# Decoder trunk step on one core: x turned on TensorE before its norm is known, the first head's work first, u and v rows by turns

## The reference

```python
xn = rms_norm(x, g_mix)
z = xn @ w_in                                  # q_a k_a v_a q_b k_b v_b g_a g_b
oa, ob, state = mix_fn(...)                    # dilated and sliding-window attention, with rotary
merged = sigmoid(ga) * (oa @ w_a) + sigmoid(gb) * (ob @ w_b)
h = x + merged @ w_o
hn = rms_norm(h, g_ffn)
# PEER, for each position and each of 8 heads:
q = (hn @ w_q)                                 # two halves of 128
s = q . sub_keys                               # 2 x 128 scores
# top 16 of each half, top 16 of their sums -> 16 experts e, gates = softmax
act = gelu(hn . u_tab[e])                      # 128 rows of 1024 per position
out = sum_e (gates * act)[e] * v_tab[e]
y = rms_norm(h + out, norm_final)
```

## Time and profile before

| | |
|---|---|
| runs, median | 2101.64 us |
| profiled execution, its own time | 2102.63 us |
| its span | 2100.8 us |
| busy: PE / DVE / GpSimd (POOL) / ACT | 1467.6 / 1215.2 / 1151.1 / 359.8 us |
| moved by DMA | 713.80 MB, mean 340 GB/s |
| share of DMA engine time: GpSimd's queue / SP's queue | 78.2% / 13.7% |
| the chain that ended last: PE / issue / DMA / POOL / DVE | 27% / 24% / 15% / 14% / 13% |

### The profile page before, as it was taken

How to read it: one execution, slowest core, us unless ns; L and a number is a source line. 1 busy time by engine, 2 the same in 40 slices (tenths; PEclk the granted TensorE clock), 3 DMA queues, 4 the chain that set the end, 5 groups by cost and what they waited for, 6 DMA issues and landing times.

```text
span 2100.8 us, 18792 instructions
## 1 busy us (share of the span) xinstructions
PE 1467.6 (70%) x5438; PEld 665.6 (32%) x5438; DVE 1215.2 (58%) x3337; ACT 359.8 (17%) x901; POOL 1151.1 (55%) x1082
## 2 busy tenths in 40 slices
PE   5999898954976687668985666664566576645457
PEld 4444344443432244333332222222222233211111
DVE  2015342287767467667644767767666767876440
ACT  2112342222221122211100111211112111100000
POOL 3020000045656657666666767677777677767664
PEclk9999999965997888778898778787877778867869
DMA  9979976578999989998999999989999999999997
GB/s 319 379 276 366 360 275 217 166 253 297 361 399 345 366 274 388 346 381 315 400 395 407 354 343 361 338 336 361 357 354 354 348 354 336 358 391 367 380 342 274
DMA packets 230423, 713.80 MB, mean 340 GB/s; under 512 B 21336, under 2 KB 49912, under 8 KB 230296
## 3 DMA queue, kind: packets, MB, share of 16 engines
q0 software_dynamic: 166912, 612.40, 78.2%
q1 hardware_dynamic: 63408, 100.19, 13.7%
HBM read 707.99 MB, written 72.65 MB: 372 GB/s over the span
## 4 chain that ended last, share of the span: by engine, by line
PE 27%; issue 24%; DMA 15%; POOL 14%; DVE 13%; another core or an unknown queue 3%; ACT 2%; POOLq 1%; SPq 0%; DVEq 0%; ACTq 0%
POOL WR L606 7%; PE bank L975 6%; DMA XS<-in_peer_u_dram,e_all 5%; DMA arena<-in_peer_u_dram,e_all 5%; POOL XS L606 5%; PE bank L866 4%; DVE XS L1363 4%; PE bank L992 4%; PE bank L1070 3%; DMA WR<-in_peer_v_dram,arena 3%; POOL arena L606 2%; PE bank L1111 2%; PE bank L1091 1%; DMA WR<-out_dram 1%
## 5 line engine op out<-in xcount | busy, mean ns | idle before, releaser
L975 PE MATMUL bank<-WR,arena 128*64 128x512 f32 x2048 | 654.4, 746 | 332.7 <-DMA WR<-in_peer_v_dram,arena 252.0
L606 POOL DMA_INDIRECT WR<-in_peer_v_dram,arena x512 | 564.0, 1101 | 277.5 <-issue 169.3
L1363 DVE SCALAR_TENSOR_TENSOR XS<-XS,GT 128x1024 f32<-128x1024 f32 x384 | 465.4, 1225 | 334.2 <-DMA XS<-in_peer_u_dram,e_all 292.1
L606 POOL DMA_INDIRECT XS<-in_peer_u_dram,e_all x384 | 419.1, 1091 | 317.5 <-issue 119.4
L975 PEld LDWEIGHTS bank<-WR,arena 128*64 128x64 f32 x2048 | 181.7, 166 | 742.2 <-issue 703.5
L1363 DVE SCALAR_TENSOR_TENSOR arena<-arena,GT 128x1024 f32<-128x1024 f32 x128 | 157.0, 1226 | 24.9 <-DMA arena<-in_peer_u_dram,e_all 18.6
L606 POOL DMA_INDIRECT arena<-in_peer_u_dram,e_all x128 | 121.8, 951 | 42.7 <-issue 37.5
L992 PE MATMUL bank<-WR,XS 128*128 128x512 f32 x256 | 117.3, 612 | 12.2 <-ACT GT L732 11.8
L866 PE MATMUL bank<-WR,XS 128*128 128x512 f32 x256 | 112.0, 595 | 0.0
L679 ACT ACTIVATE XS<-bank 128x256 f32<-128x256 f32 (+1 forms) x90 | 36.0, 404 | 425.5 <-remote 215.9
L1111 PE MATMUL bank<-XS,GT 128*128 128x128 f32 x608 | 86.7, 306 | 24.8 <-DVEq L1278 10.3
(11 more groups left out here) (208 smaller groups left out, 1679.4 us busy)
## 6 DMA issues: line engine op xcount, KB each, us to landing
out_dram<-in_cache_a_k_dram POOLq DMA_DIRECT2D x8, 4064.0 KB, 52.1
out_dram<-in_cache_a_v_dram POOLq DMA_DIRECT2D x8, 4064.0 KB, 51.9
GT<-in_w_peer_q_dram SPq DMA_DIRECT2D x17, 1024.0 KB, 8.3
WR<-in_w_in_dram SPq DMA_DIRECT2D x8, 2048.0 KB, 24.4
WR<-in_w_out_dram SPq DMA_DIRECT2D x6, 2048.0 KB
WR<-in_peer_v_dram,arena POOLq DMA_INDIRECT x512
WR<-in_w_branch_a_dram SPq DMA_DIRECT2D x6, 1024.0 KB
WR<-in_w_branch_b_dram SPq DMA_DIRECT2D x6, 1024.0 KB
```

Source lines behind the costliest of these rows:

```text
L606: nc.gpsimd.indirect_dma_start(dst, None, table, bass.IndirectOffsetOnAxis(ap=idx, axis=0))\
L975: last = nc.tensor.matmul(b[c][R * j:R * j + R, :], diag[v % 4][:, s % 4, :], V[V_AT[s]][:, c * CHUNK:(c + 1) * CHUNK], start=False, stop= ...
L1363: V_.scalar_tensor_tensor(u, u, 1.0, hidden[q // TILE_Q], ALU.mult, ALU.mult, accum_out=dots[:, s // TOPK % 4, s % TOPK:s % TOPK + 1]).the ...
```

## The change

Three things are changed.

1. ACT squares each tile of x when it lands, and PE transposes the unscaled x, all five tiles before the first projection. `rstd` is applied as the scale of ACT's evacuations instead of by DVE on x. The identity, tile 0 and `gmix` are loaded first. `sel` is copied later.
2. In steps 21 to 28 the pieces of the first choice (`CHAIN`) come first in each step. The attention of tile 1 moves to steps 25 to 28 (its `turned` stays on step 21, its `first` goes to 24), the decode rows' values are spread anew (20, 20, 25, 26, 27, 27, 28, 29), `sample_back` and `sample_own` go two steps later, and `lists`, `sums`, `pick`, `spread`, `weigh` and `index` of the very first head one step earlier. SP's loads of values and query weights are reordered to match.
3. GpSimd asks for u and v rows by turns.

```diff
@@ -71,7 +71,8 @@
     for i in range(TILES * NH):
-        x = i if i < NH else SLOT0 - NH // 2 + i - NH
+
+        x = i if i < NH else (25, 26, 26, 27, 27, 28, 28, 28)[i - NH] if i < NH + 8 else SLOT0 - 8 + i - NH
         t, hd = divmod(i, NH)
...
@@ -82,9 +83,9 @@
         elif hd == 0:
-            put(x, "turned", t)
+            put(x if t > 1 else 21, "turned", t)
             put(x if t > 1 else NH, "post", t - 1)
-            put(x, "first", t)
+            put(x if t > 1 else 24, "first", t)
         if hd == HA + 1:
...
@@ -96,12 +97,12 @@
         put(2 * b, "sample_qk", b)
-        put(20 + b, "sample_pv", b)
+        put((20, 20, 25, 26, 27, 27, 28, 29)[b], "sample_pv", b)
     put(15, "sample_soft")
     put(16, "sample_norm")
     put(17, "sample_turn")
-    put(28, "sample_back")
-    put(29, "sample_own")
+    put(30, "sample_back")
+    put(31, "sample_own")
     put(SLOT0 + 41, "post", TILES - 1)
...
@@ -120,7 +121,7 @@
                     continue
-                put(x + lag, stage, t, h)
+                put(x + lag - ((t, h) == (0, 0) and lag >= 2), stage, t, h)
     put(head_at(SAMPLE, PH - 1) + 8, "sample_turn_lists")
...
@@ -152,6 +153,8 @@
             rest.append(p)
+    if beside == "chain":
+        return sorted(pieces, key=lambda p: 0 if p[0] in CHAIN else 1)
     if beside:
...
@@ -162,15 +165,21 @@
 
+CHAIN = ("square", "norm", "hidden", "query", "query_out", "score", "score_out", "lists", "sums", "pick")
+
 
 def beside(x, pieces):
 
     names = [p[0] for p in pieces]
+    if SLOT0 - 8 <= x < SLOT0:
+        return "chain"
     return x >= SLOT0 - NH // 2 and names.count("att") <= 1 and "first" not in names and "end" not in names
 
 
 def other_order(pieces, beside):
 
+    if beside == "chain":
+        return sorted(pieces, key=lambda p: 0 if p[0] in CHAIN else 1)
     return sorted(pieces, key=lambda p: 3 if beside and p[0] in ATT else FIRST.get(p[0], 2))
...
@@ -387,12 +397,13 @@
         def _(sp):
-            for t in range(TILES):
-                sp.dma_start(GT[:, t, 0:D], x_p[t * P:(t + 1) * P, :]).then_inc(S["x_in"], 16)
+            sp.dma_start(ident[:, :], ident_d).then_inc(S["id_in"], 16)
+            sp.dma_start(GT[:, 0, 0:D], x_p[0:P, :]).then_inc(x_in[0], 16)
+            sp.dma_start(gmix[:, :], g_mix.rearrange("(k p) -> p k", p=P), allow_slow_non_contiguous=True).then_inc(S["id_in"], 16)
+            for t in range(1, TILES):
+                sp.dma_start(GT[:, t, 0:D], x_p[t * P:(t + 1) * P, :]).then_inc(x_in[t], 16)
             sp.wait_ge(S["x_zero"], 1)
-            sp.dma_start(GT[0:DEC, SAMPLE, 0:D], x_s).then_inc(S["x_in"], 16)
-            sp.dma_start(ident[:, :], ident_d).then_inc(S["id_in"], 16)
-            sp.dma_start(gmix[:, :], g_mix.rearrange("(k p) -> p k", p=P), allow_slow_non_contiguous=True).then_inc(S["id_in"], 16)
+            sp.dma_start(GT[0:DEC, SAMPLE, 0:D], x_s).then_inc(x_in[SAMPLE], 16)
             sp.dma_start(w_ring[1][:, :, 0:2 * WK], w_in_v[:, :, KB:KB + 2 * WK]).then_inc(S["w_in1"], 16)
...
@@ -518,11 +529,14 @@
             branch_weights(1, 1)
-            for b in range(3, 7):
-                values(b)
+            values(3)
+            values(4)
             query_weights(1)
+            values(5)
+            values(6)
+            query_weights(2)
             values(7)
-            for n in range(2, 6):
+            for n in range(3, 6):
                 query_weights(n)
...
@@ -643,26 +657,27 @@
                         q = piece[1]
-                        if q < UQ:
-                            for j in range(QUAD):
+                        for j in range(QUAD):
+                            if q < UQ:
                                 fetch_u(q * QUAD + j)
-                        if LAG <= q < UQ + LAG:
-                            for j in range(QUAD):
+                            if LAG <= q < UQ + LAG:
                                 fetch_v((q - LAG) * QUAD + j)
 
         @block.scalar
         def _(act):
-            act.wait_ge(S["x_in"], XLOADS)
             act.wait_ge(S["eps"], 1)
             for t in range(ALL):
+                act.wait_ge(x_in[t], 16)
                 nc.scalar.activation(GT[:, t, D:2 * D], GT[:, t, 0:D], ACT.Square, accum_out=ss[:, t:t + 1])\
                     .then_inc(S["stat"], 1)
             act.wait_ge(S["stat"], ALL)
             nc.scalar.activation(std, ss, ACT.Sqrt, bias=epsc, scale=1.0 / D).then_inc(S["std"], 1)
 
+            act.wait_ge(S["rstd"], 1)
             for m in range(ALL):
                 act.wait_ge(full[2 + m], 1)
-                nc.scalar.activation(Z[:, m, KB:KB + 2 * WK], bank[2 + m][:, 0:2 * WK], ACT.Copy).then_inc(free[2 + m], 1)
+                nc.scalar.activation(Z[:, m, KB:KB + 2 * WK], bank[2 + m][:, 0:2 * WK], ACT.Copy, scale=rstd[:, m:m + 1])\
+                    .then_inc(free[2 + m], 1)
 
...
@@ -671,8 +686,8 @@
                     act.wait_ge(full[2 + m], 2 + c if m < TILES else 3 + 2 * c)
-                    nc.scalar.activation(Z[0:n, m, CHUNK_AT[c]:CHUNK_AT[c] + CHUNK], bank[2 + m][0:n, :], ACT.Copy)\
-                        .then_inc(free[2 + m], 1)
+                    nc.scalar.activation(Z[0:n, m, CHUNK_AT[c]:CHUNK_AT[c] + CHUNK], bank[2 + m][0:n, :], ACT.Copy,
+                                         scale=rstd[0:n, m:m + 1]).then_inc(free[2 + m], 1)
 
...
@@ -827,12 +844,12 @@
             def transpose_x(m):
-                pe.wait_ge(S["xs"], m + 1)
+                pe.wait_ge(x_in[m], 16)
                 for half in range(2):
                     if m:
                         pe.wait_ge(free[half], m)
                     for k in range(4):
-                        col = D + (4 * half + k) * P
+                        col = (4 * half + k) * P
                         last = nc.tensor.transpose(bank[half][:, k * P:(k + 1) * P], GT[:, m, col:col + P], ident[:, :])
...
@@ -844,11 +861,9 @@
 
-            pe.wait_ge(S["sel"], 4)
-            transpose_x(0)
             for m in range(ALL):
-                if m + 1 < ALL:
-                    transpose_x(m + 1)
+                transpose_x(m)
+            for m in range(ALL):
                 pe.wait_ge(free[0], m + 1)
...
@@ -867,6 +882,8 @@
                     if m == 0:
+                        if c == 0:
+                            pe.wait_ge(S["sel"], 4)
                         pe.wait_ge(free[2 + SAMPLE], 2 + 2 * c)
...
@@ -1136,14 +1153,7 @@
 
-            dve.wait_ge(S["std"], 1)
-            V_.reciprocal(rstd, std).then_inc(S["rstd"], 1)
-            dve.wait_ge(S["rstd"], 1)
-            for t in range(ALL):
-                V_.tensor_scalar(GT[:, t, D:2 * D], GT[:, t, 0:D], rstd[:, t:t + 1], None, ALU.mult).then_inc(S["xs"], 1)
             dve.wait_ge(S["id_in"], 32)
-            for j in range(4):
-                V_.tensor_copy(sel[32 * j:32 * j + 32, :], ident[32 * j:32 * j + 32, 32 * j:32 * j + DEC]).then_inc(S["sel"], 1)
             for m in range(ALL):
...
@@ -1151,6 +1161,10 @@
                         .then_inc(free[half], 1)
+            dve.wait_ge(S["std"], 1)
+            V_.reciprocal(rstd, std).then_inc(S["rstd"], 1)
+            for j in range(4):
+                V_.tensor_copy(sel[32 * j:32 * j + 32, :], ident[32 * j:32 * j + 32, 32 * j:32 * j + DEC]).then_inc(S["sel"], 1)
             for e in range(G):
```

More of the change, by code:

```diff
@@ L337, in hybrid_step_kernel @@
         free = [sem(f"free{i}") for i in range(8)]
-        for n in ("x_in", "const_in", "w_in0", "w_in1", "ab_in0", "ab_in1", "out_in0", "out_in1", "wq0_in", "gffn_in", "gfin_in",
-                  "x_zero", "copies", "stat", "std", "rstd", "xs", "rot", "rot_s", "probs", "pv", "onorm", "merged",
+        for n in ("const_in", "w_in0", "w_in1", "ab_in0", "ab_in1", "out_in0", "out_in1", "wq0_in", "gffn_in", "gfin_in",
+                  "x_zero", "copies", "stat", "std", "rstd", "rot", "rot_s", "probs", "pv", "onorm", "merged",
                   "dve", "kvzero", "q_out", "kv_in0", "kv_in1", "q_in0", "q_in1", "v_in0", "v_in1", "v_in2",
@@ L346, in hybrid_step_kernel @@
         stored = [sem(f"stored{t}") for t in range(TILES)]
+        x_in = [sem(f"x_in{t}") for t in range(ALL)]
         u_landed = [sem(f"u_landed{j}") for j in range(UR)]
@@ L361, in hybrid_step_kernel @@
         CHUNK_AT = [QA, KA, VA, QB] + [ZW + c * CHUNK for c in range(4)]
-        XLOADS, CONSTS = 16 * ALL, 16 * 14
+        CONSTS = 16 * 14
         Z_ORDER = (SAMPLE, 0, 1, 2, 3)
@@ L731, in _ @@
                         b = filled(act, "gate", at[0], 0)
-                        nc.scalar.activation(GT[:, m, c * CHUNK:(c + 1) * CHUNK], b[:, :], ACT.Sigmoid if m < TILES else ACT.Copy)\
+                        nc.scalar.activation(GT[:, m, c * CHUNK:(c + 1) * CHUNK], b[:, :], ACT.Sigmoid if m < TILES else ACT.Copy,
+                                             scale=rstd[:, m:m + 1] if m < TILES else 1.0)\
                             .then_inc(free[misc_bank("gate", at[0], 0)], 1)
@@ L736, in _ @@
```

(3 more changed lines are left out.)

## The result

The kernel after takes 2212.73 us (median of 4 runs, 2201.27 to 2217.31) where the kernel before, on the same chip, takes 2104.48 (4 runs, 2100.76 to 2109.02). The ratio is 1.0505, 95% interval 1.0454 to 1.0556: 108 us slower, where 2083 was forecast. The profiled execution took 2208.53 us, with a span of 2206.7.

The account below looks back on a forecast made before the run. Expert row fetching near the DMA limit was taken to bound three quarters of the span, PE's way to the first choice the start. 2100.8 - 12 - 12 + 5 = 2081.8, plus 1.8 outside, less 1.0 for the median: 2083; range 2048 to 2113.

Parts of the forecast that it names:

- Part 1: Start of the kernel, x turned as it lands: PE reaches the 512-column matmuls 12 us earlier, bounds 8 and 15.
- give-back of 0 to 4: Weight loads beside the cache copies may use up spare time: -4 to 0 us of the early start, kept for the range.
- Part 2: First choice's own work first: DVE uses the first row 9.7 us earlier, then 12 us from the second four; bounds 6, 16.
- three marks: Signs after both shifts: first choice written near 390 us, first sum near 406, second group of sums near 415.
- Part 3: GpSimd's u and v requests by turns: more lone sums stretch issues by 30 us, mostly swallowed by waits; +5 us, near zero.
- upper bound of 150: Extreme for u and v by turns: every one of 512 sums holds a GpSimd issue for 0.61 us, +150 us.
- Rival (a): GpSimd's v requests waiting for PE hold the u behind them: +50 us, 2128; sign, waits above 140 us; chance 0.16.
- Rival (b): Lone DVE sums hold GpSimd's request queue: +35 us, 2113; sign, a mean request of 1.2; chance 0.12.
- Rival (c): Turns make requests arrive evenly: -25 us, 2053; sign, DMA share above 0.97 from 1200 to 2000 us; chance 0.14.
- Rival (d): Early gain given back in weight and key loads and slower attention pieces: 6 us left of each early gain, 2095; chance 0.08.

Follow-up runs that it names:

- e9: The kernel before with only the change to x (turned as it lands, scales in the evacuations), requests as before; 2096.05 us, ratio 0.9938.
- e10: The kernel before with only the first choice's own work put first, x and requests as before; 2094.02 us, ratio 0.9925.
- the repeat: The kernel after with requests as before, four u then four v, run again on another chip; 2066.24 us, ratio 0.9891 to the kernel before.
- e1_blocks: The kernel after with GpSimd's requests as before, four u then four v; 2060.16 us, ratio 0.9857 to the kernel before.
- e5: The kernel after, requests by turns, with DVE's four sums behind its other pieces of each step; 2120.98 us, ratio 1.0141 to the kernel before.
- e6: The kernel after with four u then four v, and DVE's four sums last in each step; 2085.57 us, ratio 0.9982 to the kernel before.
- e7: The kernel after, requests by turns, with PE's v matmuls ahead of its other pieces of each step; 2103.84 us, ratio 1.0037 to the kernel before.
- e8: The kernel after with four u then four v, and PE's v matmuls first in each step; 2067.15 us, ratio 0.9873 to the kernel before.
- e11: The kernel after, requests by turns, with DVE's sums last and PE's v matmuls first in each step; 2196.72 us, ratio 1.0463.
- e12: The kernel after with four u then four v, DVE's sums last and PE's v matmuls first; 2076.32 us on a faster chip, ratio 1.0365.
- e16: The kernel after with four u then four v, DVE's sums last and PE's v matmuls first, run again on another chip; 2156.45 us, ratio 1.0315.
- e13: The kernel after with four v then four u, and PE's v matmuls first in each step; 1978.67 us on a faster chip, ratio 0.9873.

## Why the prediction was right in two parts and wrong in the third

**Part 1** was right. It was priced at 12 us. PE's start on the 512-column matmuls is 13.9 earlier: `gmix` landed at 5.84, not 7.8, and the five projections took 17.43, where 17.5 and 0.9 were said. The scale read from SBUF costs ACT 0.47 us in place of 0.38 and is hidden, as said. With part 1 alone the choice is 9.7 earlier where PE started on these matmuls 13.7 earlier (32.68 in e9), so 4 us are given back on the way. That is the size of the give-back of 0 to 4 kept for the range; whether a load takes it, as said, wasn't looked for. At the end it is worth 13 us (0.9915 to 0.996).

**Part 2** was right. In e10 the choice is written 20.8 us earlier, where some 20 were said of the first request, and the first sum starts at 416.59, 11.1 earlier where 9.7 was said. The three marks named for both parts were 390, 406 and 415; the trace of after has 389.39, 404.80 and 413.49. Its worth is 16 us (0.9896 to 0.9954) against 12. Both together give 30 us, and 23 in the repeat, for the predicted 24. That a microsecond off the start of the row stage is one off the end held as well: in e1_blocks the first v request is 27.6 us earlier (474.7) and the end 30, from an interval of 20 to 40.

**Part 3** is the step that failed: "+5 us, near zero, as the row that it is nearest to is the DMA share of 0.95". It is +125 us by itself, near the upper bound of 150, though that bound was worked out for another mechanism. That it lies inside is luck. The term's own mechanism was right in size: some 30 us more of GpSimd's time were said, and its requests for the prompt take 1129.6 us in after against 1104.9. What failed is the path that was put at nothing, the v request's wait for PE fed back over DVE. Three things were wrong in it.

- The price was taken from GpSimd's own time: spare of 9% against stretching. The rows show that most of the loss is not GpSimd's own time. It stood still, up to 14.83 us at once.
- The waits for PE were treated as a given amount, 110 us, that turns only make dearer. Rival (a) says so: "each such wait ends with three more issues still to do, 4.2 us". The amount itself grew, from 112 to 152 us (520 to 2160 us, with the waits called remote), since the v request's wait feeds back on its own cause. The text names the first half of the circle ("DVE ... starts its other work that much later") and the second ("the first v ... now stands ahead of three u"), each as a delay of one pass. It never asked whether DVE's other work is what PE's v matmuls stand behind.
- The DMA share of 0.95 spoke for a queue that is rarely empty. But it was read from 1200 to 2000 us, where attention, branches and output matmuls are over, and there after still shows 0.93. The loss lies in the stretch before, where this work shares the queues of DVE and PE. One window of it stood in the earlier trace rows, 1000 to 1160 us with 1.03, the fullest of all; there after falls to 0.85.

**Rival (a)** is what happened, in kind. Its own mark, waits for PE above 140 us, came in: 146.9 us, and 152 with those called remote, as the 110 of today were counted. Its price, 2128, took a quarter of 4.2 us for each wait and missed the feedback by a factor of two and a half. It had a chance of 0.16, and the range ended at 2113, below its time.

**Rival (b)**, more requests held beside the sums, is there as well, and small. Compared at the same order on DVE and PE, turns stay slower than four and four by 1.6% (e5 and e6) and 1.6% (e7 and e8), with the first loop broken, and by 1.0 to 1.5% (e11 against e12 and e16), with the second one closed: 21 to 34 us. GpSimd's 1024 requests for the prompt take 1141.8 against 1122.3 us (e5, e6), 1136.1 against 1121.2 (e7, e8), and 1151.2 against 1124.8 (e11, e16): 15 to 26 us more. The costliest groups of e7 and e8 show where, in the rows whose target is `arena`:

```profile
L620 POOL DMA_INDIRECT arena<-in_peer_u_dram,e_all x128 | 140.0, 1094 | 44.7 <-issue 37.8
```

```profile
L620 POOL DMA_INDIRECT arena<-in_peer_u_dram,e_all x128 | 122.0, 953 | 40.9 <-issue 38.2
```

A request for `arena`, the fourth u, takes 1094 ns under turns and 953 under four and four. That this stretching is the whole of the remainder is argued, not shown; what remains of the loop in e5 and e7 may be part of it.

What stretches a request can be read from all 1040 of them, sorted by what DVE did at the same time. In after the 168 beside no DVE instruction take 0.94 us on average and never over 1.01, the 615 beside a sum 1.17, up to 1.99, and the rest, beside other DVE work, 1.04. In before they are 229 with 0.94 (up to 1.01) and 480 with 1.19. So turns bring more requests beside sums, each stretched no more than before. The picture behind the bound, that a burst of sums lets the next requests go free, does not hold even for its own row: the request of 1.99 at 1747.81 lies in a burst of four sums, from 1745.47 to 1750.13. The Trainium skill, "SBUF — State Buffer", section "Who interferes with whom", infers that `tensor_tensor` with two SBUF inputs doesn't hold descriptor generation, since it takes the shared read interface alone. The rows, whose sums are another DVE operation with two SBUF inputs, disagree with that inference: in none of the kernels here did a request beside no DVE instruction take over 1.01 us, and in each one beside a sum took 1.98 us or more.

**Rival (c)**, turns pay, didn't show at all: its sign was a DMA share above 0.97 from 1200 to 2000 us, where after has 0.93 and before 0.95. **Rival (d)** shows in the 4 us of part 1 alone.

The version to keep is e1_blocks, parts 1 and 2 with the requests of before: 1.4% under the kernel before (1.1% in the repeat) and 6.2% under the kernel after (0.9857 against 1.0505). e8 and e13, both at 0.9873, can't be told from it; none is measurably below it.

Open is the residual of 21 to 34 us between turns and four and four, as above, the two long waits without a named releaser, and the some 30 us that after loses between v request 192 and the last.

## What to carry to other kernels

Where one queue issues requests that wait for two different consumers, count for each wait how many requests lie between the one that starts the chain and the one that waits for its end, and follow that chain through the in-order queues of the other engines. If it comes back to the request, the waits of the old profile don't give the price, because they grow with the change: the longest went from 6.2 to 14.83 us here. The long ones did not come in every round either, but fourteen times, where the other engines had other work in their queues. The distances tried here (eight requests, four, two, none) give an order of the losses (0, 86, 136, 150 us), not a formula. A high mean DMA share elsewhere says nothing about it: look at the stretch where other work stands in the same queues. An order changed on one engine can break the loop; changed on two, most of the loss came back.

## What was not expected of the hardware

The kernel before took 2002.6 us (median) on one chip and 2091.63 to 2107.43 on the others, a difference of 4 to 5%. Its runs on one chip spread by up to 1.5% (2072.42 to 2102.69), and the four ratios that were measured on two chips agree within 0.6%.
